# Moving the first block's 32 modulation passes from VectorE to GpSimd and ScalarE

## The reference, cut to what matters

```python
h = x
for _layer in range(DEPTH):                      # DEPTH = 1: the first block
    proj = jnp.einsum('btd,de->bte', rms_norm(h, norm_in_g), w_in)
    ...
    h = h + jnp.einsum('bte,ed->btd', mixed, w_out)
...
for l in range(DEPTH_2):                         # DEPTH_2 = 2: the second block
    mod = (jax.nn.silu(c) @ w_mod[l] + b_mod[l])[:, None, :]
    mod_c = jax.nn.silu(c_ctx) @ w_mod[l] + b_mod[l]
    sh1, sc1, ga1, sh2, sc2, ga2 = jnp.split(mod, 6, axis=-1)
    ...
    h = modulate(rms_norm_2(x, g_pre_mix[l]), sh1, sc1)       # h * (1 + sc1) + sh1
```

## Time and profile before

| | us |
|---|---|
| median of three runs | 1617.15 |
| the profiled execution, whole | 1621.3 |
| its span, first to last instruction | 1619.5 |
| PE busy in the span | 1594.7 (98%) |
| DVE busy | 1235.4 (76%) |
| ACT busy | 857.6 (53%) |
| GpSimd busy | 0.2 (0%) |

### The profile page before, as it was taken

The page is one execution under the profiler, slowest core; times in us unless marked ns, Lnnn a source line. Parts: engine busy times, 40 slices in busy tenths (PEclk is TensorE's granted clock), DMA queues, the critical chain, the costliest instruction groups (busy, mean ns, idle before and its releaser), DMA issues.

```text
span 1619.5 us, 25155 instructions
## 1 busy us (share of the span) xinstructions
PE 1594.7 (98%) x9772; PEld 1418.5 (88%) x9772; DVE 1235.4 (76%) x2143; ACT 857.6 (53%) x1403; POOL 0.2 (0%) x4
## 2 busy tenths in 40 slices
PE   9999999999999999999999999999999999999998
PEld 9999788778888878889888888889788989989997
DVE  7999877875788798967888886347766776778874
ACT  7776555564334444347444442348563466576654
POOL 0000000000000000000000000000000000000000
PEclk9999999999999999999999999999999999999999
DMA  8767752232334345543555556324522455555554
GB/s 331 253 208 252 247 164 87 97 130 67 77 112 166 105 166 193 203 151 105 146 148 201 207 208 234 104 79 144 105 92 71 124 171 157 190 174 177 188 199 140
DMA packets 80230, 258.02 MB, mean 159 GB/s; under 512 B 14448, under 2 KB 18800, under 8 KB 79472
## 3 DMA queue, kind: packets, MB, share of 16 engines
q1 hardware_dynamic: 74352, 248.02, 46.6%
q10 hardware_dynamic: 5760, 8.39, 1.5%
HBM read 255.31 MB, written 1.07 MB: 158 GB/s over the span
## 4 chain that ended last, share of the span: by engine, by line
PE 70%; DVE 17%; ACT 6%; issue 4%; DMA 3%; ACTq 0%; DVEq 0%; SPq 0%
PE bank L838 58%; DVE w_lo L2102 4%; DVE mod_w L2157 2%; PE bank L1034 2%; DMA w_raw<-in_weights 2%; PE bank L1308 2%; ACT w_hi L1420 2%; PE bank L1228 2%; PE bank L1212 2%; PE bank L1200 1%; DVE att L2790 1%; PE bank L1294 1%; DVE bank L2788 1%; DVE probT L2157 1%; PE bank L876 0%
## 5 line engine op out<-in xcount | busy, mean ns | idle before, releaser
L2102 DVE TENSOR_TENSOR w_lo<-w_raw,w_hi 128x1024 fp32r<-128x1024 f32 (+1 forms) x356 | 427.3, 1209 | 219.0 <-ACT w_hi L1420 217.8
L1420 ACT ACTIVATE w_hi<-w_raw 128x1024 fp32r<-128x1024 f32 (+1 forms) x356 | 369.0, 1046 | 304.4 <-PE bank L838 247.6
L838 PE MATMUL bank<-hT_hi,w_hi 128*128 128x512 f32 (+1 forms) x960 | 346.3, 361 | 0.0
L838 PE MATMUL bank<-hT_hi,w_lo 128*128 128x512 f32 (+1 forms) x960 | 337.2, 351 | 0.0
L838 PE MATMUL bank<-hT_lo,w_hi 128*128 128x512 f32 (+1 forms) x960 | 337.2, 351 | 0.0
L838 PEld LDWEIGHTS bank<-hT_hi,w_hi 128*128 128x128 f32 x960 | 182.2, 190 | 19.7 <-issue 1.3
L838 PEld LDWEIGHTS bank<-hT_hi,w_lo 128*128 128x128 f32 x960 | 182.2, 190 | 18.9
L838 PEld LDWEIGHTS bank<-hT_lo,w_hi 128*128 128x128 f32 x960 | 182.3, 190 | 18.7 <-issue 1.0
L2157 DVE SCALAR_TENSOR_TENSOR mod_w<-mod_w,c_rows 128x1024 f32<-128x1024 f32 x102 | 124.2, 1218 | 6.8 <-DMA mod_w<-in_mod_weights 6.6
L838 PE MATMUL bank<-w_hi,hT_hi 128*128 128x512 f32 x272 | 111.0, 408 | 0.0
L3153 DVE SCALAR_TENSOR_TENSOR conv<-bank,vec,conv 128x510 f32<-128x510 f32 (+1 forms) x176 | 103.0, 611 | 3.2
(11 more groups left out here) (429 smaller groups left out, 3075.9 us busy)
## 6 DMA issues: line engine op xcount, KB each, us to landing
w_raw<-in_weights SPq DMA_DIRECT2D x356, 512.0 KB, 4.3
mod_w<-in_mod_weights SPq DMA_DIRECT2D x102, 512.0 KB, 3.9
nbias<-in_window_bias ACTq DMA_DIRECT2D x32, 128.0 KB, 3.2
resid_c<-in_ctx ACTq DMA_DIRECT2D x2, 1024.0 KB, 6.9
gain_mix<-gain_rows SPq DMA_DIRECT2D x3, 512.0 KB, 5.5
gain_ffn<-gain_rows SPq DMA_DIRECT2D x3, 512.0 KB, 4.3
c_rows<-in_conditions SPq DMA_DIRECT2D x1, 1024.0 KB, 8.6
gatew<-in_gate_weights SPq DMA_DIRECT2D x1, 1024.0 KB, 11.2
```

The source lines that it names most:

```text
L838: mm = pe.matmul(held[key][:, oc], st, mv_, start=(opens and k == 0 and t == 0 and i == 0), stop=(closes and k == tiles - 1 and t == 2), s ...
L1420: a.activation(w_hi[:, p % RING, :, used], w_raw[:, p % RING, :].rearrange("p (k n) -> p k n", k=KP)[:, :, used], ACT.Copy).then_inc(hi_re ...
L2102: v.tensor_tensor(w_lo[:, p % RING, :, used], w_raw[:, p % RING, :].rearrange("p (k n) -> p k n", k=KP)[:, :, used], w_hi[:, p % RING, :, ...
```

## The change

`sums(p)` and the GpSimd program are new, the 32 passes leave DVE, and the early loads get other places in the stream.

- GpSimd multiplies a block with a vector (TENSOR_TENSOR, 128x1024) into `probT` or onto the slot. It waits for the block's load, for its own pass before (`mod_times`), and, where it writes `probT`, until the job before is summed (`mod_used`).
- ACT sums the product's rows with an ACTIVATE of the kind Copy with a sum output. The sums of job i stand right behind the rounding of piece `mod_after()[i] + 4`. ACT waits there for GpSimd (`mod_times`), and its last sum of a job frees the slot for SP.
- DVE's generator of passes skips the first 22 jobs; 32 passes in 21 places are removed. DVE still adds the bias after waiting for all 22 jobs.

```diff
-    at = [8, 9, 10, 12, 15, 18, 21, 24, 27, 30, 34, 37, 40, 42, 43, 44]
-    at += [51, 52, 54, 54, 56, 57]
+    at = [8, 11, 14, 17, 20, 23, 26, 28, 30, 32, 34, 36, 38, 40, 42, 44]
+    at += [45, 47, 48, 50, 51, 53]
...
+def early_passes():
+    return [(i, m, s, s == sets[-1]) for i, (m, sets) in enumerate(mod_jobs()[:EARLY_MODS]) for s in sets]
...
                     hi_done[0] += 1
+                    sums(p)
+
+            def sums(p):
+                passes = early_passes()
+                while summed[0] < len(passes) and mod_after()[passes[summed[0]][0]] + 4 <= p:
+                    i, m, s, closes = passes[summed[0]]
+                    slot, _, _ = mod_place(i)
+                    product = mod_slot[slot] if closes else junk_of_mod(m)
+                    act.wait_ge(mod_times, summed[0] + 1)
+                    a.activation(product, product, ACT.Copy, accum_out=modT[:, 0, m, s:s + 1])\
+                        .then_inc(*((mod_used, 1) if closes else A.next()))
+                    summed[0] += 1
...
+        @block.gpsimd
+        def _(pool):
+            g = nc.gpsimd
+            pool.wait_ge(*c_ready.at(0))
+            for k, (i, m, s, closes) in enumerate(early_passes()):
+                slot, count, _ = mod_place(i)
+                pool.wait_ge(mod_loaded[slot], 16 * count)
+                if not closes and i:
+                    pool.wait_ge(mod_used, i)
+                if k:
+                    pool.wait_ge(mod_times, k)
+                g.tensor_tensor(mod_slot[slot] if closes else junk_of_mod(m), mod_slot[slot], c_rows[:, s, :], ALU.mult)\
+                    .then_inc(mod_times, 1)
...
                 for i, (m, sets) in enumerate(mod_jobs()):
+                    if i < EARLY_MODS:
+                        continue
...
-            dve.wait_ge(*c_ready.at(0))
-            mod_ops(1)
             split_lo(10)
-            mod_ops(1)
...
-            mod_ops(5)
             split_lo(39)
...
-            mod_ops(2)
             ret_lo(6)
             split_lo(57)
-            mod_ops(1)
             ret_lo(7)
-            mod_ops(1)
             mod_bias(0, 0, 16, 2, EARLY_MODS)
```

More of the change, by code:

```diff
@@ L524, in build @@
     mod_used = es.enter_context(nc.semaphore("mod_used"))
+    mod_times = es.enter_context(nc.semaphore("mod_times"))
     gain_stored = es.enter_context(nc.semaphore("gain_stored"))
@@ L1406, in build @@
         hi_done = [0]
+        summed = [0]
         @block.scalar
@@ L2151, in modulations @@
                     dve.wait_ge(mod_loaded[slot], 16 * count)
-                    if i:
-                        dve.wait_ge(mod_used, i)
+                    dve.wait_ge(mod_used, i)
                     for s in sets:
@@ L2330, in _ @@
                 lru_input(n)
-            mod_ops(2)
             lru_input(HEADS - 1)
             split_lo(23)
-            mod_ops(4)
             split_lo(24)
             split_lo(25)
-            mod_ops(1)
             split_lo(26)
```

## The result

The changed kernel takes 1643.63 us (median of 4 runs, 1643.01 to 1648.23), the kernel before, on the same chip, 1617.39 us. The ratio is 1.0165, with a 95% interval of 1.0152 to 1.0177: slower by 26 us. Forecast were 1621.2 us and, at the top of the range, 1630. The direction was right, the size was not. The profiled execution stands at 1648.23 us, 4.6 above its median, as that of before stood 4.15 above; so places in the two profiles can be set against each other, but such differences are those of two executions and not of two medians.

What follows compares the result with a forecast made beforehand. PE was taken to bound the first block, DVE handing over w_lo just in time; +9.8 + 0.5 - 6.3 = +4.0 us on the 1617.15 median gave 1621.2 us, own range 1617 to 1627, wider range 1611.5 to 1630.

Steps and rivals of the forecast that it cites:

- What bounds the kernel: First block, 206 us: PE busy, DVE full; PE waits of 3.1 and 1.4 us plus 3.2 of lower clock give 7.7.
- What leaves DVE: 32 passes, 36.5 us of DVE time; PE's two waits for w_lo would give 1.4 us, of which 0.8 is left.
- What comes to ACT: 32 sums, 36 us; eight of them ahead of the first head's onrm make PE stand still there, +3.8 us.
- What comes to GpSimd: Products of 1.9 us exclude DVE operations with two SBUF operands: +9.8 us for the first stretch (with ACT's delay), +0.5 later.
- my halving rule: 30 to 120 us: half of DVE's excess falls ahead of ACT's chain; then the larger delay plus half the smaller, +9.8 us.
- the stretch from 120 to 190 us: The 12 passes left make 65 of 70 us beside DVE's other work; that fits, +0.5 us for a bad moment.
- the old wait: PE's 3.1 us wait for ACT's normalised context, 192.6 to 195.7 us; the lower clock behind it costs 3.2 us.
- What the moved loads do: At the end of the first block, no modulation loads hold weight pieces 57 to 59; context wait and lower clock go, -6.3 us.
- The rival with a held reading side and a longer pass: An operation holds SBUF reading for all its length, a pass takes 2.2 us: +10.1 us, 1627.2 us; chance 0.18.
- No contention: GpSimd and DVE do not disturb each other, only ACT's chain counts: -3.8 us, 1613.3 us; chance 0.25.
- That ACT would wait for products: From a pass of some 2.9 us on, ACT waits for products of jobs 7 to 9, pushing the time above 1630.
- POOL's 55 to 75 us of busy time: A sign that the forecast is right: POOL, with no GpSimd arithmetic before, is busy 55 to 75 us.

Runs made afterwards that it cites:

- E1: Changed kernel with products cut to 8 of 1024 columns and the 32 row sums on ScalarE left out: 1612.40 us, ratio 0.9964 to the kernel before.
- E2: Changed kernel without the 32 GpSimd products; ScalarE sums raw weights at the same places instead: 1617.60 us, ratio 0.9996 to the kernel before.
- E4: Changed kernel with each product cut into four GpSimd instructions of 128x256, nothing left out: 1633.38 us, ratio 1.0094 to the kernel before.
- E3: Changed kernel with all 32 whole products on GpSimd but the row sums on ScalarE left out: 1638.27 us, ratio 1.0123 to the kernel before.
- E8: Changed kernel with the load table of the kernel before, last sums behind piece 59, nothing left out: 1648.96 us, ratio 1.0184 to the kernel before.
- E7: Kernel before, passes still on DVE, with modulation loads 16 to 19 moved earlier and their passes one piece earlier: 1619.78 us, ratio 1.0011.
- E11: Changed kernel with each product held back until DVE finished w_lo of the second or third piece behind its load: 1637.84 us, ratio 1.0122.
- E6: Changed kernel with each GpSimd product replaced by filling the product tile with zeros: 1617.37 us, ratio 0.9993 to the kernel before.
- E5: Changed kernel with each GpSimd product replaced by one copy of the raw weights, sums kept: 1617.36 us, ratio 0.9992 to the kernel before.

## Why the prediction was wrong, step by step

*What bounds the kernel.* Right: PE has little to give, and what DVE is late with decides. But the 7.7 us to give were read from the profiled execution, 4.15 us above the median, and then taken off the median. Of the runs of before beside E1, the fastest took 1616.61 and the slowest 1619.47 us; the profiled one took 1621.3, with a mean clock of 0.997. The stretch at the lower clock, 3.2 us of the 7.7, need not be in the median.

*What leaves DVE.* 36.5 us forecast from rows; by the stretch up to the next stage 34.6. Right.

*What comes to ACT*, +3.8 us at the first `onrm`. In E2, the sums without products, ACT began `onrm` at 108.17 and PE turned it at 108.90, 2.9 us later than before and 4.3 later than in E1 (104.6), which is the run to compare with. The place was right and the size near; of the 5.2 us that the sums cost in all, the later heads, which I took to have room, have 0.9 at most. In the changed kernel PE does not wait for the first `onrm`: DVE is later.

*What comes to GpSimd*, +9.8 and +0.5 us: this is the step that failed. The mechanism I chose, that the two never read SBUF at once, is what the traces show. What failed is its price: three terms were off. First, the pass: 1.9 us by a row of ACT, 2.34 measured. My own stretch sum with 2.34 is 53.5 + 6.4 + 46.8 = 106.7, 16.7 too many, which by my halving rule gives 18.6 us; the first head's turn was 14.8 us late where I had 9.8. The Trainium skill's 2.6 cycles for each element ("GPSIMD Engine Reference", section "Elementwise — side-by-side cycle accounting"), an estimate of 2.2 us, was nearer; the runs give 2.08 ns a column between 512 and 1024 columns ((2.337 - 1.271) / 512). Second, the stretch from 120 to 190 us. I compared sums of busy time, 65 of 70, and called it fitting. From the first head's turn to the last's the kernel lost another 17.5 us (32.3 - 14.8). Products left over from the first stretch came in a burst, and in turns a short operation pays a whole product, on the chain that ends in PE's next `w_lo` (8.3 us in one wait). E4 shows the price of long turns: with shorter ones, and longer holding, 10.3 us less. How the 17.5 us divide between the burst and products elsewhere stays open, since E3 and E8 lose as much in all without it. Third, the clock. I counted 3.2 us won behind the old wait and nothing lost behind new ones. PE's busy time over the same work rose from 199.5 to 206.0 us, 6.4 of the 26.2.

*What the moved loads do*, -6.3 us: the size came out, the cause is not shown. From the last head's turn to the next stage the kernel won back 32.3 - 26.2 = 6.1 us between the two profiles. E1's profile wins 6.7 us there and 9.4 in all, its median only 6.0, so that the forecast size also fits E1's median is partly luck. Moving four loads earlier under a full DVE (E7) wins nothing, since `w_lo` is late by itself; E8 shows that modulation loads in SP's queue can hold a weight piece back as well. How much of the gain is the loads' and how much DVE's relief stays open. SP's new waits for sums did little: they are 14.5 us in E2, 7.7 the longest, where PE waited 0.8 us for a `w_hi` in all.

*The sum.* First stretch +14.8 for +9.8, second +17.5 for +0.5, end -6.1 for -6.3: 26.2 us for 4.0. The rival with a held reading side and a longer pass (1627.2) had the mechanism and nearly the pass, and 15.9 us for the first stretch; it failed by the same second stretch. No contention (1613.3) is refuted by E3. That ACT would wait for products, which I had for the top of the range, was not it in the changed kernel, though it came in E4 and E11: what ACT waits for is DVE, its head statistics and its gating of `xc`. The two waits, up to 235 us:

```profile
ACT bnst L1529 <- DVE att L2262: 14.1, 6, 5.1
ACT mix_hi L1562 <- DVE xc L2327: 10.9, 6, 2.1
```

POOL's 55 to 75 us of busy time became 83.8, part of it waiting for DVE.

No version that makes the modulation in full beats the kernel before. E1 shows 6 us to be had, with the new table, if the passes cost DVE and ScalarE nothing; a GpSimd product costs DVE more than the pass.

## What to carry to other kernels

Before work goes from DVE to GpSimd, list what DVE does meanwhile: here every operation with two SBUF operands that met a GpSimd product waited it out, however short it was itself (2.5 us for 0.42), so the price is counted in turns on the chain and not in sums of busy time. If GpSimd must read, try short instructions in place of long ones; in E4 they were better by 10.3 us although they took longer in all. And where a change brings new waits of PE, add the slow matmuls behind each; where it takes one away, first see which engine frees the slot that the transfer waited for.

## What the runs showed of the hardware

- GpSimd on 128 rows of f32: a fill of 1024 columns 0.95 us, a copy 1.04, a product of 256, 512 and 1024 columns 0.715, 1.27 and 2.34 us.
- A fill left `w_lo` at 1220 ns (E6); a copy (E5) or a product (the changed kernel) keeps it out for its whole length, and is kept out by it.
- The clamp of `xc`, one SBUF operand, 128x2048 in 1214 ns, twice the pace of the others, took 3216 ns beside products, in one meeting: it is blocked too. The Trainium skill, "SBUF — State Buffer", section "Who interferes with whom", says that `tensor_scalar` can enter a two-port mode of DVE and then contends with GpSimd; the trace agrees.
- The scan with two SBUF operands is blocked like the others (690 to 1185 ns); batch statistics and operations with an operand from PSUM are not (277 ns in the changed kernel and 279 in E1 for a batch statistic, 416 and 418 for `sT`).
- ScalarE's operations kept their lengths beside GpSimd: a sum is 1.046 us in the changed kernel and in E2, where GpSimd does nothing, a rounding 1.053 us in the changed kernel and 1.058 in E1.
